# A four-layer hybrid decoder trunk: one more seven-product pair in three feed-forward blocks, and inverse roots by logarithm and exponential

## The chip, the cores and the metric

The kernel runs on 1 core of one Trainium2 chip. The metric is the device time of one execution in microseconds. Five engines work side by side, each through its own instruction list in order: TensorE (PE: matrix products; PEld is its weight load), VectorE (DVE), ScalarE (ACT), GpSimd (POOL) and SyncE (SP, which issues DMA transfers). They meet at semaphores: an instruction waits until a counter has reached a value, another adds to the counter when it is done.

## The reference

`x` has 512 tokens of 1024 features, float32. There are two layers, and each is `x + 0.5*FFN(norm(x))`, a token mixer, and another half-step FFN: four feed-forward blocks in all, numbered 0 to 3 here.

```
rms_norm(x, g)  = x * rsqrt(mean(x*x) + 1e-6) * g
swiglu(x)       = (silu(x @ w_gate) * (x @ w_up)) @ w_down      # 1024 -> 2816 -> 1024
layer 0 (even)  : FFN 0; dilated attention and causal pooling; FFN 1
layer 1 (odd)   : FFN 2; mLSTM, four heads, with an rms_norm of each head's output; FFN 3
```

## The kernel before

Features lie on the 128 partitions, tokens along the free dimension. All large products are float32 in accuracy: each operand is split into a high part (ScalarE copies it to the fp32r type: HI, XH, BF, ASH, HH) and a low part (value minus high part, on VectorE or GpSimd: LO, XL, BFL, ASL, HL), and three matmuls are summed: high by high, high by low, low by high.

**A feed-forward block** (`block_ffn(f, ...)`, written once for each engine) has 22 pairs of 128 hidden features. A pair has a gate and an up tile, `units` 2p and 2p+1, and each unit has 1024 input features, eight blocks of 128.

- A *plain* pair (p < `PLAIN[f]`) multiplies both units directly: 2 x 8 x 3 = 48 matmuls of 512 tokens (`products`, lines 579 to 581).
- A *block* pair (p >= `PLAIN[f]`) is a two by two product with seven multiplications instead of eight (`block(p)`, `product`, lines 656 to 658): 7 x 4 x 3 = 84 matmuls of 256 tokens. The halves are the input features and the tokens. Its tokens are sums of quarters of the normed x (`form`, `form_split`: BFR, BF, BFL, made once per FFN, four steps a = 0 to 3), and its weights are sums of quarter tiles in ASR, four per pair. Two of the four come from DMA: SP loads two quarters (`load_pair`), and GpSimd issues a transfer that adds the gate's left half to both (`add_pair`, an accumulating DMA, L2254). The other two are made on VectorE (`sums_second`, `sums_third`, L1664 and L1670). `sums_split(p, 0)` and `(p, 1)` make ASH on ScalarE and ASL on VectorE (L1676). After the products VectorE joins the partial results: `mid_two`, `mid_five`, `mid_three`, `whole_up`, `whole_gate`.
- In PE's order the seven products of a block pair are called here *one, seven, five, six, up-left, three, last*. *One* needs the pair's first LO (and, in the first block pair, all four split forms), *seven* needs `sums_split(p, 0)`, *six* needs `sums_split(p, 1)` and the copy of *one*, *last* needs `mid_two` and `mid_five` of the same pair.
- After every pair come `gate(p)` (bank times RSTD, VectorE), `silu(p)` (ScalarE), a product with RSTD (GpSimd, L2262, signals `sr_ready`), `up(p)` (VectorE, L1695), `h_high(p)` (ScalarE, L1179) and the low part HL on GpSimd (L2264).
- From a pair on, PE puts an *early* piece of the down projection behind each block pair (`early`, lines 709 to 711), with weights from DRAW/DHI/DLO (`load_early`, `early_split`). Its first pair is `PLAIN[f]`. The rest of the down projection follows at the end.

`PLAIN` is (5, 4, 3, 3): 17, 18, 19 and 19 block pairs, 73 in all.

**The norm.** The sum of squares is turned into a row on PE (L635, L636, into AUX, which is bank 4), behind the first three of eight steps of unit 2 or 3. ScalarE takes the root (L1123, `std_ready`), VectorE the reciprocal (L1610, `rstd_ready`). This is done six times. In the mLSTM a root (L1452) and a reciprocal (L2091) do the same for each of four heads. PE's first block pair waits for `std_ready` since product *seven* writes bank 4.

**What sets the order.** Every engine's list is written out by hand. The start of `block_ffn` has three variants: f == 0, f == 1 and the rest. In f = 2 and 3 the forms 0 and 1 are made behind the previous stage (`forms_behind`), forms 2 and 3 at the start of the block; in f = 1 all four are made at the start. Block 1 starts near 534 us, block 2 near 880 us, block 3 near 1606 us of the span.

## Time and profile before

| what | before |
|---|---|
| median of 3 runs | 1954.88 us (1954.53 to 1955.82) |
| the profiled execution's own time | 1955.77 us |
| its span, first to last instruction | 1954.0 us |
| PE busy | 1948.1 us, 100% |
| DVE busy | 1397.9 us, 72% |
| ACT busy | 851.6 us, 44% |
| POOL busy | 527.3 us, 27% |
| granted PE clock | 1.00 (2.4 GHz) |
| DMA | 265.92 MB, 136 GB/s |

A share of busy time is a mean over the whole span. PE's is a busy time with modelled ends, so starts of matmuls are the better measure of its pace. An instruction's duration in the timeline runs from its start to its visible end; the next one on the same engine can start about 0.08 us (VectorE) or 0.10 us (ScalarE) before that end.

### The profile page before, as it was taken

To read this page: it belongs to the slowest core of one execution; us is meant where nothing else is said; L and a number is where in the kernel's file an instruction comes from. 1 tells how busy PE (TensorE), PEld (TensorE's weight loads), DVE (VectorE), ACT (ScalarE), POOL (GpSimd) and SP (SyncE) were. 2 spreads that over 40 slices of the span, in tenths; PEclk is the share of its full clock that TensorE was granted. 3 is DMA by queue.
4 is the path that set the end of the run, shared out by engine and by line. 5 is a ranking of instruction groups with operands and counts; after the bars stand their busy time and mean duration, and the time that the engine had idled before them with its cause. 6 is when DMAs were issued, how large, how long until landed. Compare 5 with 4: busy or idle time off the path is not lost.

```text
span 1954.0 us, 28996 instructions
## 1 busy us (share of the span) xinstructions
PE 1948.1 (100%) x11722; PEld 1707.3 (87%) x11722; DVE 1397.9 (72%) x1882; ACT 851.6 (44%) x1230; POOL 527.3 (27%) x394
## 2 busy tenths in 40 slices
PE   9999999999999999999999999999999999999999
PEld 7999998877789999988999998877777888999997
DVE  7877776554588877768877776773458657877773
ACT  6443333535554344345433444442546345333431
POOL 1322222142223322223322322200015413322221
PEclk9999999999999999999999999999999999999999
DMA  6556663351346666545666653232200235666653
GB/s 211 155 164 171 173 168 95 119 181 55 88 126 176 174 172 167 147 129 145 178 166 172 181 151 114 97 96 88 76 1 1 87 116 160 177 173 168 178 141 107
DMA packets 112469, 265.92 MB, mean 136 GB/s; under 512 B 10321, under 2 KB 22865, under 8 KB 112337
## 3 DMA queue, kind: packets, MB, share of 16 engines
q1 hardware_dynamic: 92336, 225.72, 35.3%
q0 software_dynamic: 19856, 38.28, 12.5%
q8 instruction: 93, 1.52, 0.3%
q14 instruction: 40, 0.32, 0.0%
q10 hardware_dynamic: 144, 0.09, 0.0%
HBM read 259.32 MB, written 4.72 MB: 135 GB/s over the span
## 4 chain that ended last, share of the span: by engine, by line
PE 98%; DVE 1%; DMA 0%; issue 0%; ACT 0%; SPq 0%; POOL 0%; DVEq 0%
PE BANKS L656 12%; PE BANKS L658 12%; PE BANKS L657 12%; PE BANKS L579 11%; PE BANKS L580 11%; PE BANKS L581 11%; PE BANKS L709 6%; PE BANKS L710 6%; PE BANKS L711 6%; PE BANKS L1022 2%; PE BANKS L850 1%; PE BANKS L852 1%; PE BANKS L851 1%; PE BANKS L999 1%; PE BANKS L1005 1%; PE BANKS L813 1%
## 5 line engine op out<-in xcount | busy, mean ns | idle before, releaser
L656 PE MATMUL BANKS<-BF,ASH 128*128 128x256 f32 x876 | 248.0, 283 | 0.0
L658 PE MATMUL BANKS<-BF,ASL 128*128 128x256 f32 x876 | 247.9, 283 | 0.0
L657 PE MATMUL BANKS<-BFL,ASH 128*128 128x256 f32 x876 | 247.9, 283 | 0.0
L579 PE MATMUL BANKS<-XH,HI 128*128 128x512 f32 x624 | 245.7, 394 | 0.7 <-DVE XL L1593 0.3
L1657 DVE TENSOR_TENSOR LO<-RING,HI 128x1024 fp32r<-128x1024 f32 (+2 forms) x204 | 216.3, 1060 | 41.2 <-ACT HI L1160 39.9
L580 PE MATMUL BANKS<-XL,HI 128*128 128x512 f32 x624 | 243.2, 390 | 0.0
L581 PE MATMUL BANKS<-XH,LO 128*128 128x512 f32 x624 | 243.0, 389 | 0.0
L1173 ACT ACTIVATE TMP<-TMP 128x512 f32<-128x512 f32 x88 | 55.7, 633 | 406.4 <-DVE TMP L1686 406.4
L2262 POOL TENSOR_TENSOR TMP<-TMP,RSTD 128x512 f32<-128x512 f32 x88 | 132.0, 1499 | 365.3 <-ACT TMP L1173 365.3
L2254 POOL DMA_DIRECT2D ASR<-gu_dram x73 | 88.1, 1219 | 387.5 <-DMA ASR<-gu_dram 381.5
L709 PE MATMUL BANKS<-HH,DHI 128*128 128x512 f32 x488 | 190.7, 391 | 0.0
L710 PE MATMUL BANKS<-HL,DHI 128*128 128x512 f32 x488 | 190.6, 391 | 0.0
L1160 ACT ACTIVATE HI<-RING 128x1024 fp32r<-128x1024 f32 (+2 forms) x204 | 171.4, 876 | 42.3 <-DMA RING<-down_dram 21.4
L711 PE MATMUL BANKS<-HH,DLO 128*128 128x512 f32 x488 | 189.8, 389 | 0.0
L1676 DVE TENSOR_TENSOR ASL<-ASR,ASH 128x1024 fp32r<-128x1024 f32 x146 | 181.6, 1246 | 0.0
L2264 POOL TENSOR_TENSOR HL<-TMP,HH 128x512 fp32r<-128x512 f32 x88 | 139.0, 1580 | 146.6 <-ACT HH L1179 146.6
L1584 DVE TENSOR_TENSOR LO<-RING,HI 128x1024 fp32r<-128x1024 f32 x66 | 85.3, 1294 | 121.6 <-ACT HI L1102 121.5
L656 PEld LDWEIGHTS BANKS<-BF,ASH 128*128 128x128 f32 x876 | 168.2, 192 | 0.0
L657 PEld LDWEIGHTS BANKS<-BFL,ASH 128*128 128x128 f32 x876 | 168.2, 192 | 0.0
L658 PEld LDWEIGHTS BANKS<-BF,ASL 128*128 128x128 f32 x876 | 168.2, 192 | 0.0
L658 PE MATMUL BANKS<-XH,LO 128*128 128x256 f32 x584 | 165.3, 283 | 0.0
L657 PE MATMUL BANKS<-XL,HI 128*128 128x256 f32 x584 | 165.2, 283 | 0.0
(249 smaller groups left out, 4875.5 us busy)
## 6 DMA issues: line engine op xcount, KB each, us to landing
RING<-gu_dram SPq DMA_DIRECT2D x174, 512.0 KB, 3.9
ASR<-gu_dram SPq DMA_DIRECT2D x146, 256.0 KB, 2.9
ASR<-gu_dram POOLq DMA_DIRECT2D x73, 512.0 KB, 6.9
DRAW<-down_dram SPq DMA_DIRECT2D x40, 512.0 KB, 3.7
RING<-oin_dram SPq DMA_DIRECT2D x32, 512.0 KB, 3.5
RING<-down_dram SPq DMA_DIRECT2D x32, 384.0 KB, 3.2
DRAW<-down_dram SPq DMA_DIRECT2D x24, 384.0 KB, 3.7
RING<-ein_dram SPq DMA_DIRECT2D x16, 512.0 KB, 3.6
```

Of the source, the lines that this page charges most:

```text
L579: pe.matmul(PS[bank][:], HI[j][:, c], hi(k), start=(n == 0), stop=False)
L580: pe.matmul(PS[bank][:], HI[j][:, c], lo(k), start=False, stop=False)
L581: last = pe.matmul(PS[bank][:], LO[j][:, c], hi(k), start=False, stop=(n == len(order) - 1))
L656: pe.matmul(out, w_hi[:, c], x_hi(k), start=(k == 0), stop=False)
L657: pe.matmul(out, w_hi[:, c], x_lo(k), start=False, stop=False)
L658: last = pe.matmul(out, w_lo[:, c], x_hi(k), start=False, stop=(k == 3))
L709: pe.matmul(bank, DHI[:, col], HH[:, h % 8, :], start=(k == 0), stop=False)
L710: pe.matmul(bank, DHI[:, col], HL[:, h % 8, :], start=False, stop=False)
L711: last = pe.matmul(bank, DLO[:, col], HH[:, h % 8, :], start=False, stop=(h == tiles[-1]))
L1160: act.activation(HI[j][:, cols], RAW[j][:, cols], ACT.Copy).then_inc(hi_ready, 1)
L1657: dve.tensor_tensor(LO[j][:, cols], RAW[j][:, cols], HI[j][:, cols].bitcast(F32), ALU.subtract).then_inc(lo_ready, 1)
L1676: dve.tensor_tensor(ASL[:, p % 2, 2 * i:2 * i + 2, :], ASR[:, p % 2, 2 * i:2 * i + 2, :], ASH[:, p % 2, 2 * i:2 * i + 2, :].bitcast(F32), ...
```

## The change

- `PLAIN` becomes (5, 3, 2, 2): pair 3 of block 1 and pair 2 of blocks 2 and 3 become block pairs. A new tuple `EARLY_FROM = (5, 4, 3, 3)` keeps the first early piece of the down projection where it was, so the new block pair has none behind it.
- The lists at the start of blocks 1, 2 and 3 are reordered on ScalarE and VectorE. For the first block pair of these blocks the sums and splits of the next pair move (`ahead`), and its three `mid` steps stand ahead of the split of the next unit. In blocks 1 to 3 PE waits for the free gate bank ahead of product *five* instead of ahead of *one*.
- In blocks 2 and 3 the last `form_split` stands ahead of the norm on both engines.
- Block 2's first two accumulating transfers are issued by GpSimd between the squares of the previous block instead of after them.
- All norms and the head factor: `Sqrt` on ScalarE and `reciprocal` on VectorE become `Ln` and `Exp` with scale -0.5, both on ScalarE. `rstd_ready` takes the place of `std_ready` everywhere.

```diff
-PLAIN = (5, 4, 3, 3)
+PLAIN = (5, 3, 2, 2)
+EARLY_FROM = (5, 4, 3, 3)
...
@@ PE, block(p)
-                    pe.wait_ge(bank_free, n + 2)
+                    if f == 0:
+                        pe.wait_ge(bank_free, n + 2)
                     if p == PLAIN[f]:
-                        pe.wait_ge(std_ready, r + 1)
+                        pe.wait_ge(rstd_ready, r + 1)
...
                     product(PS[4][:, low], *summed(p, 0), form(1)).then_inc(seven_done, 1)
+                    if f:
+                        pe.wait_ge(bank_free, n + 2)
...
@@ ScalarE
             def norm(r):
                 act.wait_ge(norm_sum, r + 1)
-                act.activation(RSTD[:], AUX[:], ACT.Sqrt, scale=1.0 / DM, bias=EPST[:]).then_inc(std_ready, 1)
+                link(act.activation(RSTD[:], AUX[:], ACT.Ln, scale=1.0 / DM, bias=EPST[:]))
+                act.activation(RSTD[:], RSTD[:], ACT.Exp, scale=-0.5).then_inc(rstd_ready, 1)
...
@@ ScalarE, start of block 1
-                    split(6, whole)
                     silu(0, 1.0)
                     form_split(f, 3)
-                    split(7, whole)
+                    split(2 * first, whole)
+                    sums_split(first, 0)
                     h_high(0)
                     silu(1, 1.0)
-                    sums_split(first, 0)
+                    sums_split(first, 1)
+                    split(2 * first + 1, right)
                     h_high(1)
-                    silu(2, 1.0)
-                    split(2 * first, whole)
-                    h_high(2)
@@ ScalarE, start of blocks 2 and 3
                     form_inputs(f, 3)
+                    form_split(f, 3)
                     norm(now)
-                    split(4, whole)
-                    form_split(f, 3)
+                    split(2 * first, whole)
+                    sums_split(first, 0)
+                    sums_split(first, 1)
                     silu(0, 1.0)
-                    split(5, whole)
-                    sums_split(first, 0)
+                    split(2 * first + 1, right)
                     h_high(0)
...
@@ VectorE
             def norm(r):
-                dve.wait_ge(std_ready, r + 1)
-                dve.reciprocal(RSTD[:], RSTD[:]).then_inc(rstd_ready, 1)
                 dve.wait_ge(rstd_ready, r + 1)
@@ VectorE, start of block 1
                     form_split(f, 2)
-                    split(6, whole)
+                    sums_second(first)
+                    sums_third(first)
                     up(0)
                     gate(1)
                     form_split(f, 3)
-                    split(7, whole)
-                    up(1)
-                    gate(2)
-                    sums_second(first)
-                    sums_third(first)
-                    up(2)
@@ VectorE, start of blocks 2 and 3
                     form(f, 3)
+                    form_split(f, 3)
                     norm(now)
-                    split(4, whole)
                     gate(0)
-                    form_split(f, 3)
-                    up(0)
-                    split(5, whole)
-                    gate(1)
                     sums_second(first)
                     sums_third(first)
-                    up(1)
@@ VectorE, then in blocks 1 to 3
                 split(2 * first, whole)
                 sums_split(first, 0)
+                if f == 1:
+                    up(1)
                 sums_split(first, 1)
+                if f >= 2:
+                    up(0)
                 gate(first - 1)
                 split(2 * first + 1, right)
+                if f:
+                    sums_second(first + 1)
+                    sums_third(first + 1)
                 up(first - 1)
...
@@ GpSimd
+                    if f == 1 and m in (2, 3):
+                        add_pair(2, PLAIN[2] + m - 2)
```

## Rows read from the trace of the kernel before

**Rows 1.** The head of the page and its first part, busy times.
```profile
span 1954.0 us, 28996 instructions
PE 1948.1 (100%) x11722; PEld 1707.3 (87%) x11722; DVE 1397.9 (72%) x1882; ACT 851.6 (44%) x1230; POOL 527.3 (27%) x394
```
**Rows 2.** Waits of PE: line and releaser, us in total, times, longest.
```profile
PE BANKS L609 <- POOL HH L2330: 1.4, 1, 1.4
PE BANKS L1022 <- DVE VL L2108: 0.4, 1, 0.4
```
**Rows 3.** Timeline of PE in block 2: start, duration; operation; count.
```profile
902.35 0.39 PE L579 MATMUL BANKS<-XH,HI 128*128 128x512 f32 x1
...
913.23 0.28 PE L656 MATMUL BANKS<-XH,HI 128*128 128x256 f32 x1
...
923.30 0.40 PE L709 MATMUL BANKS<-HH,DHI 128*128 128x512 f32 x1
```
**Rows 4.** Groups of VectorE and ScalarE by line and shape: count, busy us, mean ns.
```profile
L1676 DVE TENSOR_TENSOR ASL<-ASR,ASH 128x1024 fp32r<-128x1024 f32 x146 | 181.6, 1246 | 0.0
...
L1686 DVE TENSOR_TENSOR TMP<-BANKS,RSTD 128x512 f32<-128x512 f32 x88 | 60.7, 690 | 2.5
...
L1657 DVE TENSOR_TENSOR LO<-RING,HI 128x512 fp32r<-128x512 f32 x73 | 49.7, 680 | 0.0
...
L1610 DVE RECIPROCAL RSTD<-RSTD 128x512 f32<-128x512 f32 x6 | 20.1, 3350 | 17.4 <-ACT RSTD L1123 17.4
...
L1160 ACT ACTIVATE HI<-RING 128x1024 fp32r<-128x1024 f32 x99 | 104.0, 1051 | 19.3 <-DMA RING<-gu_dram 8.6 <-DMA RING<-oin_dram 5.8 <-DMA RING<-ein_dram 4.9
L1173 ACT ACTIVATE TMP<-TMP 128x512 f32<-128x512 f32 x88 | 55.7, 633 | 406.4 <-DVE TMP L1686 406.4
```
**Rows 5.** Timeline of ScalarE at block 1's norm.
```profile
552.58 1.28 ACT L1123 ACT_TABLE_LOAD   x1
553.88 0.69 ACT L1123 ACTIVATE RSTD<-BANKS,EPST 128x512 f32<-128x512 f32 x1
...
558.44 1.28 ACT L1173 ACT_TABLE_LOAD   x1
```
**Rows 6.** Timeline of VectorE and GpSimd in block 1, 566 to 572 us.
```profile
566.05 1.21 DVE L1639 TENSOR_TENSOR BFL<-BFR,BF 128x1024 fp32r<-128x1024 f32 x1
...
566.27 2.14 POOL L2264 TENSOR_TENSOR HL<-TMP,HH 128x512 fp32r<-128x512 f32 x1 [3.90 <-ACT HH L1179]
...
567.18 2.31 DVE L1657 TENSOR_TENSOR LO<-RING,HI 128x1024 fp32r<-128x1024 f32 x1
...
568.37 2.27 POOL L2262 TENSOR_TENSOR TMP<-TMP,RSTD 128x512 f32<-128x512 f32 x1
570.67 0.69 DVE L1695 TENSOR_TENSOR TMP<-BANKS,TMP 128x512 f32<-128x512 f32 x1 [1.18 <-POOL TMP L2262]
```
**Rows 7.** Timeline of GpSimd, block 1, a product with VectorE idle.
```profile
581.98 1.29 POOL L2262 TENSOR_TENSOR TMP<-TMP,RSTD 128x512 f32<-128x512 f32 x1 [3.56 <-ACT TMP L1173]
```
**Rows 8.** Chain that ended last, around block 1's second block pair: start, us, what.
```profile
600.32 0.43 DVE MID L1701
...
600.77 0.43 DVE MID L1707
...
601.25 0.38 PE BANKS L656
```
**Rows 9.** Timeline of ScalarE in the mLSTM stage: an exponential, then a logarithm.
```profile
1383.01 0.63 ACT L1405 ACTIVATE TMP<-TMP 4x512 f32<-4x512 f32 x1
1383.65 1.28 ACT L1406 ACT_TABLE_LOAD   x1
```
**Rows 10.** Timeline of VectorE and ScalarE at the start of block 2.
```profile
894.69 0.42 DVE L1634 SCALAR_TENSOR_TENSOR BFR<-BFR,MID 128x256 f32<-128x256 f32 x1
...
898.83 1.06 ACT L1160 ACTIVATE HI<-RING 128x1024 fp32r<-128x1024 f32 x1 [4.00 <-DMA RING<-gu_dram]
```
**Rows 11.** Timeline of ScalarE at the start of block 3.
```profile
1619.60 0.69 ACT L1123 ACTIVATE RSTD<-BANKS,EPST 128x512 f32<-128x512 f32 x1 [4.47 <-PE BANKS L636]
1622.85 1.06 ACT L1160 ACTIVATE HI<-RING 128x1024 fp32r<-128x1024 f32 x1 [2.57 <-DMA RING<-gu_dram]
```

More of the change, by code:

```diff
@@ L287, in trunk @@
         sq_hi, sq_lo = sem("sq_hi"), sem("sq_lo")
-        norm_sum, std_ready, rstd_ready = sem("norm_sum"), sem("std_ready"), sem("rstd_ready")
+        norm_sum, rstd_ready = sem("norm_sum"), sem("rstd_ready")
         small_ready = sem("small_ready")
@@ L311, in trunk @@
         vh_ready, pth_ready, ptl_ready = sem("vh_ready"), sem("pth_ready"), sem("ptl_ready")
-        num_done, den_abs, num_sq, ssq_step, tstd_ready, num_read = (
-            sem(n) for n in ("num_done", "den_abs", "num_sq", "ssq_step", "tstd_ready", "num_read"))
+        num_done, den_abs, num_sq, ssq_step, factor_root, num_read = (
+            sem(n) for n in ("num_done", "den_abs", "num_sq", "ssq_step", "factor_root", "num_read"))
         column_sum, factor_ready, den_ready = sem("column_sum"), sem("factor_ready"), sem("den_ready")
@@ L364, in plain_bank @@
         def plain_bank(f, n):
-            return n + 1 if f < 2 and 4 <= n < 7 else n % 4
+            return n + 1 + f if f < 2 and 4 <= n < 7 - f else n % 4
         def block_count(f, p):
@@ L377, in early_index @@
         def early_index(f, p):
-            return p - PLAIN[f] - (p > ALONE[f])
+            return p - EARLY_FROM[f] - (p > ALONE[f])
         def has_early(f, p):
@@ L383, in leads @@
         def leads(f, p):
-            return has_early(f, p) and (p == PLAIN[f] or not has_early(f, p - 1))
+            return has_early(f, p) and not has_early(f, p - 1)
         def early_pairs(f):
@@ L461, in block_ffn @@
                     p = n // 2 - 1
-                    if n == plain + 1:
+                    if n == plain + 1 and has_early(f, PLAIN[f]):
                         load_early(PLAIN[f])
-                    elif n % 2 and p == ALONE[f]:
+                    elif n % 2 and p >= PLAIN[f] and leads(f, p + 1):
                         load_early(p + 1)
@@ L641, in bias_part @@
                     pe.wait_ge(bias_ready, 3)
-                    pe.wait_ge(std_ready, 2)
+                    pe.wait_ge(rstd_ready, 2)
                 if n >= 4:
@@ L1252, in block_ffn @@
                     form_inputs(f, 3)
+                    form_split(f, 3)
                     norm(now)
-                    split(4, whole)
-                    form_split(f, 3)
+                    split(2 * first, whole)
+                    sums_split(first, 0)
+                    sums_split(first, 1)
                     silu(0, 1.0)
-                    split(5, whole)
-                    sums_split(first, 0)
+                    split(2 * first + 1, right)
                     h_high(0)
-                    silu(1, 1.0)
-                    split(2 * first, whole)
-                    h_high(1)
-                sums_split(first, 1)
-                split(2 * first + 1, right)
+                if f == 0:
+                    sums_split(first, 1)
+                    split(2 * first + 1, right)
                 silu(first - 1, 1.0)
@@ L1268, in block_ffn @@
                     copy_one(p)
-                    if p == first:
+                    ahead = f and p == first
+                    if f and p == first + 1:
+                        silu(p - 1, -1.0)
+                    if ahead:
+                        split(2 * nxt, whole)
+                        sums_split(nxt, 0)
+                        sums_split(nxt, 1)
+                    if not has_early(f, p - 1):
                         h_high(p - 1)
+                    if p == first and has_early(f, p):
                         early_split(p)
-                    elif not has_early(f, p - 1):
-                        h_high(p - 1)
-                    if nxt:
+                    if ahead:
+                        split(2 * nxt + 1, right)
+                    elif nxt:
                         split(2 * nxt, whole)
@@ L1281, in block_ffn @@
                         split(NU + 1, late)
-                    if p == ALONE[f]:
+                    if leads(f, p + 1):
                         early_split(p + 1)
@@ L1285, in block_ffn @@
                         early_split(p)
-                    silu(p, -1.0)
+                    if not ahead:
+                        silu(p, -1.0)
                     if has_early(f, p):
@@ L1451, in root @@
                         act.wait_ge(factor_ready, h + 1)
-                        act.activation(RSTD[:], RSTD[:], ACT.Sqrt).then_inc(tstd_ready, 1)
+                        link(act.activation(RSTD[:], RSTD[:], ACT.Ln))
+                        act.activation(RSTD[:], RSTD[:], ACT.Exp, scale=-0.5).then_inc(factor_root, 1)
                 def square_numerator(h, c):
@@ L1853, in block_ffn @@
                     elif nxt:
-                        sums_second(nxt)
-                        sums_third(nxt)
+                        if p == first:
+                            mid_two(p)
+                            mid_five(p)
+                            mid_three(p)
+                        else:
+                            sums_second(nxt)
+                            sums_third(nxt)
                         dve.wait_ge(sum_made, 2 * block_count(f, nxt) + 2)
                         split(2 * nxt, whole)
-                        mid_two(p)
-                        mid_five(p)
-                        mid_three(p)
+                        if p > first:
+                            mid_two(p)
+                            mid_five(p)
+                            mid_three(p)
                         sums_split(nxt, 0)
@@ L2087, in head_factor, with root_ready @@
                                              ALU.add).then_inc(factor_ready, 1)
-                def invert_factor(h):
-                    dve.wait_ge(tstd_ready, h + 1)
-                    link(dve.reciprocal(RSTD[:], RSTD[:]))
+                def root_ready(h):
+                    dve.wait_ge(factor_root, h + 1)
                 def scale_numerator(h, c):
@@ L2142, in odd_mixer @@
                     value_low(h, 2)
-                    invert_factor(h - 1)
+                    root_ready(h - 1)
                     weighted(h, 0)
```

23 lines of the change are left out of this document (12 added, 11 removed).

## The prediction

> **What bounds the kernel now.** First the page's busy shares: PE is busy for 1948.1 of 1954.0 us, VectorE for 72% [rows 1]. Then PE's waits: the two longest are 1.4 us at the very start and 0.4 us in the mLSTM stage [rows 2]. So no wait of any size can be removed; time comes only out of PE's own work, and every microsecond by which another engine makes PE wait is added in full. Third, PE's pace by starts: from 902.35 to 913.23 lie the 48 matmuls of one plain pair, 10.88 us (0.227 each); from 913.23 to 923.30 the 84 of a block pair, 10.07 us (0.120 each) [rows 3]. The last view is the chain around PE's one wait inside the feed-forward blocks: in block 1 VectorE's `mid_five` ends at 601.20 and PE's product *last*, whose predecessor started at 600.90, starts at 601.25 instead of 601.02 [rows 8]. There VectorE is the engine that comes late, just behind the stretch where the change puts more on it.
>
> **The gain.** Three pairs change kind: 3 x (10.88 - 10.07) = 2.43 us less PE work. It is there only if the inputs come in time. Each new block pair starts 10.88 us earlier than the first one did: at 567.25 (578.13 - 10.88) in block 1, 902.35 in block 2, 1628.27 in block 3.
>
> **The work added.** A plain pair costs VectorE two splits of 1.14 us and two bank reads of 0.60 (next start after the durations of rows 4, less 0.08): 3.5. A block pair costs it one and a half splits (1.74), two sums (1.32), two sum splits (2.28), three mids (1.15), two joins (1.3), two bank reads (1.2): 9.0. So +5.5 us of VectorE per changed pair, -3.35 for the reciprocal [rows 4]. The form steps (1.53 each, 1.14 for each split) stay in the same stretch.
>
> **The root.** Before: table load, Sqrt 0.69, reciprocal 3.35 on VectorE. After: Ln 0.69, another table load 1.28, Exp about 0.65. That the pair needs two loads I read from the mLSTM stage, where an Exp is followed at once by a load of 1.28 us for the Ln [rows 9]. RSTD is there 2.7 us after the sum instead of 4.4: 1.7 earlier; but ScalarE is later by 1.9 us, and VectorE, freed of 3.35 us, waits for ScalarE instead. The Trainium skill (ScalarE: Activation LUTs, "Table sets: the hidden batching unit") says that ln and then exp cost one load, since one set has both. The trace has a case in the other order only, with two loads. By the skill's rule each norm would be 1.3 us shorter: a rival, below.
>
> **The meeting with GpSimd.** At 566.27 a GpSimd operation starts while a VectorE split is under way until 567.18: it takes 2.14 us, against 1.29 when VectorE is idle [rows 6, 7]. VectorE's next split, 567.18, takes 2.31 instead of 1.21, and ends 1.1 us behind GpSimd's end at 568.41; GpSimd's next, from 568.37, takes 2.27 [rows 6]. So these two take turns when VectorE's operands lie in SBUF, and each turn lost costs 1.2 us. Reads of a bank don't show it. I lay the new order out with that, instruction by instruction, in the durations above. The same layout of the old order puts block 1's second block pair at 592.7 (592.4 in the trace), so I trust it to some 0.3 us per block.
>
> **Block 1, laid out.** Ln starts at 553.88 like the Sqrt [rows 5], load to 555.9, Exp to 556.5, the high part of unit 5 (1.05) to 557.4. VectorE: LO of unit 5 to 558.6, gate 0 to 559.2, form 3 to 560.7, form split 2 to 561.8; the two sums of pair 3 with one lost turn to 564.3; up 0 and gate 1 to 565.5; form split 3 to 566.7; then LO of unit 6, behind GpSimd's HL 0, to 569.0. PE wanted it at 567.25: **1.8 us**. The first sum split loses the next turn (sr 1) and ends at 571.3, *seven* wanted it at 570.5: 0.9. ScalarE copies *one* only behind silu 2, which waits for gate 2 at 573.6: *six* is 0.5 late. Then the next pair's split and sum split, behind `mid_three`: *seven* of pair 4 is 0.6 late. `mid_five` of pair 4: 0.36, of pair 5: 0.31. Sum 4.4 (4.38), against 0.56 in my layout of the old order, less 0.81 for the pair: **+3.0 us**. The moved wait for the gate bank costs nothing: up 1 ends at 571.9, *five* starts at 572.8.
>
> **Block 2.** Form 3 ends at 895.11 [rows 10]. ScalarE's last form split now stands ahead of the norm, so it waits for that until 895.15, ends at 896.1, and only then come load, Ln, load, Exp: RSTD at 900.1, where the old order had it at 898.4. Here the new root is later, not earlier. Gate 0, two sums, LO of unit 4: 903.3; PE wanted it at 902.35: **1.0 late**. ScalarE: high part of unit 4, two sum splits, silu's table load, silu 0 at 904.4, GpSimd's product to 906.7, up 0 to 907.4: *five* wanted it at 906.2: **1.3 late**. Then *six* 0.1, `mid_five` 0.4, and LO of unit 6, which loses a turn to HL 1, 1.1; in the next two pairs 0.1 and 0.3. Sum 4.2 - 0.81 = **+3.4 us**. The two accumulating transfers that go out sooner should take away ScalarE's 4.00 us of waiting for unit 4's weights, which ended at 898.83 [rows 10]; but ScalarE gets to this split only at 900.0. Worth 0 here, and 0 if the weights come as late as before.
>
> **Block 3.** The same lists, but form 3 is ready 3 us before the norm's sum, which comes at 1619.6 [rows 11]. Ln, load and Exp end at 1622.2; unit 4's weights landed at 1622.85 before [rows 11] and set ScalarE's start. LO of unit 4 at 1625.4 (wanted 1628.3), up 0 at 1629.7 (wanted 1631.1): both in time. Only LO of unit 6 is 0.24 late, and the mids 0.37. 0.6 - 0.81 = **-0.2 us**.
>
> **The rest.** Block 0's norm: VectorE freed, ScalarE 1.9 us later, hidden under its wait of 2 us for weights behind it: 0. The norms ahead of the mixers: 0, PE reads RSTD's result 6 us later at least. mLSTM roots: ScalarE's value copy comes 1.9 us later and is read in time by 0.3 us, VectorE loses 3.35 us of work per head; PE waits there for neither: 0, between -0.5 and +1. A table load more for the q/k root falls into idle time: 0. PE's wait for `rstd_ready` instead of `std_ready`: 10 us early in block 1, 2.2 in block 2, covered by LO.
>
> **Sum.** +3.0 + 3.4 - 0.2 = +6.2 us. Against the profiled execution's 1955.77 (span 1954.0, 1.77 around it) that is 1962.0 us, span 1960.2. The median of the runs is 0.89 lower, so the forecast is **1961.1 us**. What a measurement can tell from no change is 0.2%, 3.9 us: 1951.0 to 1958.8.
>
> **Rivals.**
> - *The turns don't fall on the path (not slower).* VectorE and GpSimd take turns as in rows 6, but in the new order GpSimd's operations slip into VectorE's waits. For: the reciprocal goes, and in the trace many GpSimd operations meet an idle VectorE [rows 7]. Against: in block 1 VectorE now has no gap between 557 and 587. With no lost turn in either order the layout gives -0.8, +1.3, -0.8, and the old order's 0.4 us of stall goes: -0.7, 1954.2 us. It decides from the point where LO of unit 6 (block 1) is there by 567.3. Chance 0.17.
> - *All arrives in time.* -2.43 and the old stalls of 0.4: 1952.1 us. For it block 2's form 3 would have to be ready sooner too, and nothing in the change does that. Chance 0.05.
> - *Ln and Exp in one table set.* RSTD 1.3 us earlier, by the layout +1.75 in block 1 and +2.1 in block 2, -0.2 in block 3: +3.7, 1958.5 us. Against it stand rows 9. This is the skill's rule named above. Chance 0.08.
> - *Block 3 goes like block 2.* The weights of unit 4 or the sums of pair 2 land later than the 1622.85 of rows 11, since the pair's accumulating transfers are issued at the old place there, and the pair starts 10.88 us sooner. From 2.9 us of delay on PE waits. At block 2's price, +9.8 in all: 1964.7 us. Chance 0.12.
> - The forecast: 0.56, own range 1959 to 1963.5. The rest, 0.02, is beyond all of these.
>
> Range 1953.8 to 1964.8: it takes in the first, third and fourth rival. Faster by over 0.2%: 0.05 (the second rival with gains in the mixers I don't see). Within 0.2%: 0.17 + 0.05 and the larger part of the one-set case, with the forecast's lower tail: 0.31. Slower: 0.64.
>
> **What would show it.** In the profile after: 84-matmul stretches of 10.07 us from pair 3, 2 and 2 on; a table load between Ln and Exp at each norm; PE waiting on LO near 567 and 903 for 1 to 2 us and on up 0 near 906; the start of block 1's pair 6 near 609.9 (606.9 before) and of block 2's pair 5 some 3.4 us later again; none of it in block 3; no new waits in the mixers. It is wrong if PE's first block pair of block 1 starts within 0.3 us of 567.25, if the load between Ln and Exp is missing, or if VectorE's split of unit 6 runs undisturbed.

## The result, and the profile after

The changed kernel takes 1964.07 us (median of 5 runs, 1962.99 to 1964.44) against 1955.08 for the kernel before (5 runs); the ratio is 1.0043, 95% interval 1.0031 to 1.0055, that is 6 to 11 us more. Forecast were 1961.1, range 1953.8 to 1964.8, slower with chance 0.64: the direction and the main mechanism are right, the size is 3.0 us short. The number lies above the forecast's own range (1959 to 1963.5) and close to the 1964.7 of the rival on block 3; what tells the two apart is the table of stages below, not the number. The profiled execution is the shortest of the five, 1962.99, with a span of 1961.3 (1954.0 before).

First the head and the busy times of the page after, beside [rows 1], and PE's waits after (line and releaser, us in total, times, longest), beside [rows 2]:

```profile
span 1961.3 us, 29291 instructions
PE 1949.0 (99%) x11830; PEld 1711.4 (87%) x11830; DVE 1388.9 (71%) x1899; ACT 875.0 (45%) x1258; POOL 533.1 (27%) x397
```
```profile
PE BANKS L657 <- DVE LO L1667: 2.7, 2, 1.4
PE BANKS L610 <- POOL HH L2345: 1.4, 1, 1.4
PE BANKS L657 <- DVE ASL L1686: 1.3, 3, 0.5
PE BANKS L657 <- DVE TMP L1705: 1.0, 1, 1.0
PE BANKS L657 <- DVE MID L1717: 0.5, 3, 0.2
```

VectorE has 9 us less work than before, and this execution is 7.3 us longer: its reciprocals are gone, but the work that was added is due sooner. The waits stand where the prediction put them: the splits LO of block 1 and block 2 (2.7 us), up 0 (1.0), the sum splits (1.3), the mids. The timeline of PE shows the four long ones (start, duration, operation, idle time ahead of it and what ended it):

```profile
567.71 0.39 PE L657 MATMUL BANKS<-XH,HI 128*128 128x256 f32 x1 [1.39 <-DVE LO L1667]
...
569.93 0.38 PE L657 MATMUL BANKS<-BF,ASH 128*128 128x256 f32 x1 [0.54 <-DVE ASL L1686]
...
906.88 0.39 PE L657 MATMUL BANKS<-XH,HI 128*128 128x256 f32 x1 [1.33 <-DVE LO L1667]
...
911.02 0.39 PE L657 MATMUL BANKS<-BF,ASH 128*128 128x256 f32 x1 [1.00 <-DVE TMP L1705]
```

The scale for all that follows is PE's own timeline. I take the start of the same matmul in both traces (the norm matmuls, and one *early* matmul well inside each feed-forward block) and subtract. How much the distance grows from one mark to the next is what a stage costs, freed of how the execution began (up to the middle of block 0 every other kernel here is 0.5 to 1.2 us ahead of the profiled execution of before). In us, pairs of marks in order of time:

```
                  block 1   1 to 2   block 2   mLSTM   block 3
forecast            +3.0      0        +3.4      0      -0.2
changed kernel      +2.9     +1.2      +3.9     +0.5    -0.2
```

"1 to 2" runs from the early pairs of block 1 to block 2's norm. Two measures of a wait are used below: the idle time of the profile's rows, and the distance of two starts of PE less the usual 0.12 or 0.23 us, which comes out some 0.16 us longer for the same wait (1.39 and 1.55 on LO in block 1). In block 1 all such excesses of starts come to 4.2 us against 0.4 before; less the pair's 0.81 that is the +2.9. Two terms that stood in the sum with 0 are not 0 (1 to 2 and mLSTM), and they are the larger part of what was missing.

The second table load is there at each of the six norms. ScalarE at block 2's norm, after:

```profile
898.51 1.06 ACT L1146 ACTIVATE BF<-BFR 128x1024 fp32r<-128x1024 f32 x1 [2.33 <-DVE BFR L1644]
899.59 1.28 ACT L1127 ACT_TABLE_LOAD   x1
900.88 0.69 ACT L1127 ACTIVATE RSTD<-BANKS,EPST 128x512 f32<-128x512 f32 x1
901.59 1.28 ACT L1128 ACT_TABLE_LOAD   x1
902.88 0.63 ACT L1128 ACTIVATE RSTD<-RSTD 128x512 f32<-128x512 f32 x1
```

The step is as forecast: the form split stands ahead of the norm and waits 2.33 us for VectorE. The splits that lose their turn to GpSimd in block 1 are there too. VectorE, then GpSimd:

```profile
565.34 2.31 DVE L1667 TENSOR_TENSOR LO<-RING,HI 128x1024 fp32r<-128x1024 f32 x1
567.58 2.31 DVE L1686 TENSOR_TENSOR ASL<-ASR,ASH 128x1024 fp32r<-128x1024 f32 x1
...
564.43 2.14 POOL L2277 TENSOR_TENSOR HL<-TMP,HH 128x512 fp32r<-128x512 f32 x1 [2.62 <-ACT HH L1184]
566.52 2.27 POOL L2275 TENSOR_TENSOR TMP<-TMP,RSTD 128x512 f32<-128x512 f32 x1
```

### The profile page after: what moved, and what is told of

The parts are those of the page before. It is cut to its first block and busy times, and to the rows that moved or that the text cites. A ratio compares the mean times of both kernels' runs of the same rounds, so it can differ in the third digit from the quotient of the medians.

```text
span 1961.3 us, 29291 instructions
## 1 busy us (share of the span) xinstructions
PE 1949.0 (99%) x11830; PEld 1711.4 (87%) x11830; DVE 1388.9 (71%) x1899; ACT 875.0 (45%) x1258; POOL 533.1 (27%) x397
## 5 line engine op out<-in xcount | busy, mean ns | idle before, releaser
L657 PE MATMUL BANKS<-BF,ASH 128*128 128x256 f32 x912 | 258.9, 284 | 2.5 <-DVE ASL L1686 1.3
L659 PE MATMUL BANKS<-BF,ASL 128*128 128x256 f32 x912 | 258.1, 283 | 0.0
L658 PE MATMUL BANKS<-BFL,ASH 128*128 128x256 f32 x912 | 258.1, 283 | 0.0
L580 PE MATMUL BANKS<-XH,HI 128*128 128x512 f32 x576 | 227.0, 394 | 1.0 <-DVE LO L2210 0.3
L581 PE MATMUL BANKS<-XL,HI 128*128 128x512 f32 x576 | 224.6, 390 | 0.0
L582 PE MATMUL BANKS<-XH,LO 128*128 128x512 f32 x576 | 224.3, 389 | 0.0
L1686 DVE TENSOR_TENSOR ASL<-ASR,ASH 128x1024 fp32r<-128x1024 f32 x152 | 189.9, 1251 | 0.0
L657 PEld LDWEIGHTS BANKS<-BF,ASH 128*128 128x128 f32 x912 | 175.0, 192 | 3.6 <-DVE ASL L1686 1.9
L658 PEld LDWEIGHTS BANKS<-BFL,ASH 128*128 128x128 f32 x912 | 175.1, 192 | 0.0
L657 PE MATMUL BANKS<-XH,HI 128*128 128x256 f32 x608 | 171.9, 283 | 2.7 <-DVE LO L1667 2.7
```

Of the source, the lines that this page charges most:

```text
L580: pe.matmul(PS[bank][:], HI[j][:, c], hi(k), start=(n == 0), stop=False)
L581: pe.matmul(PS[bank][:], HI[j][:, c], lo(k), start=False, stop=False)
L582: last = pe.matmul(PS[bank][:], LO[j][:, c], hi(k), start=False, stop=(n == len(order) - 1))
L657: pe.matmul(out, w_hi[:, c], x_hi(k), start=(k == 0), stop=False)
L658: pe.matmul(out, w_hi[:, c], x_lo(k), start=False, stop=False)
L659: last = pe.matmul(out, w_lo[:, c], x_hi(k), start=False, stop=(k == 3))
```

## The experiments

Five kernels take the change apart, four alter one thing in the changed kernel, two follow from what these showed, and one repeats the changed kernel. All but the last are built with three switches: `NEW` names the blocks whose pair changes kind (a block that isn't in it keeps the old order), `ROOT` chooses the roots, `SOONER` the place of the transfers. The code shown is what is different in effect, shortened at each `...`; the lines of the switches themselves stand there only where they say it best. Runs of before beside them: 1955.1 to 1955.5 us, medians of 15 to 21.

### The parts

**The accumulating transfers at their old place**, the rest of the change kept.

```diff
-                if f != 2:
-                    for p in (PLAIN[f], PLAIN[f] + 1):
-                        add_pair(f, p)
+                for p in (PLAIN[f], PLAIN[f] + 1):
+                    add_pair(f, p)
...
-                    if f == 1 and m in (2, 3):
-                        add_pair(2, PLAIN[2] + m - 2)
```

> The changed kernel with one part undone: GpSimd issues block 2's first two accumulating transfers again behind all eight squares of block 1. My theory: in the changed kernel the two issues at 873.6 and 875.6 us hold GpSimd between the squares and stretch two VectorE steps (2.77 and 2.15 us), so VectorE is late at the start of block 2 and PE waits twice there (0.4 and 0.35 us excess). Undone, block 2's norm comes 1.2 us sooner relative to block 1's last pair, about as in the kernel before, and the rest of block 2 stays at +3.9 us: total 1.2 us less than the changed kernel (about 1962.5 to 1963). Rival: the weights of unit 4 come later then and cost as much or more in block 2 as was won: total unchanged or up to 1 us more.

Measured: 1961.86 us, ratio 1.0035 [1.0023, 1.0048]. By stages: block 1 +2.5, 1 to 2 **0.0**, block 2 +3.5, mLSTM +0.5, block 3 -0.3. So issuing them sooner costs 1.2 us between the blocks and buys nothing in block 2. (Block 1, the same code, differs by 0.4; see the landings below.)

**The roots alone**: old pairs, old transfers, Ln and Exp everywhere.

```diff
-PLAIN = (5, 3, 2, 2)
+NEW = ()
+ROOT = 'exp'
+SOONER = False
+PLAIN = tuple(n - (f in NEW) for f, n in enumerate((5, 4, 3, 3)))
```

> The kernel before with the roots alone changed: Ln and Exp instead of Sqrt and reciprocal, PLAIN and all orders as before. My layout: the 0.4 us of waits in block 1 go (-0.5 us), blocks 2 and 3 unchanged, +0.3 to +0.5 us in the mLSTM stage, where ScalarE's copy of v2 comes 1.9 us later: within 0.5 us of the kernel before. Rival: the second table load is what costs the changed kernel its time; then this one is 3 us or more slower than before.

Measured: 1955.14 us, ratio 1.0000 [0.9991, 1.0010]. Block 1 -0.4, mLSTM +0.5, the rest within 0.1.

**Block 3's pair alone**, with the new roots and the old transfers.

```diff
-PLAIN = (5, 3, 2, 2)
+NEW = (3,)
+ROOT = 'exp'
+SOONER = False
+PLAIN = tuple(n - (f in NEW) for f, n in enumerate((5, 4, 3, 3)))
```

> The changed kernel with blocks 1 and 2 as before (4 and 3 plain pairs, old orders) and the transfers at the old place; only block 3 has its new block pair, and the roots are Ln and Exp. My layout: block 3 -0.2 us, roots as in the run beside it: 1954.4 to 1955.2, no difference to before that can be measured, and the whole loss of the changed kernel gone. Rival: block 3 loses time too once it isn't hidden behind a later start: 1957 or more.

Measured: 1954.93 us, ratio 1.0000 [0.9990, 1.0009]. Block 1 -0.3, mLSTM +0.5, block 3 +0.25 with three PE waits of 0.2 to 0.3 us. Even here, where nothing is late by more than that, small waits pay the pair's 0.81 us [rows 3] back.

**The change with Sqrt and reciprocal kept.**

```diff
-                link(act.activation(RSTD[:], AUX[:], ACT.Ln, scale=1.0 / DM, bias=EPST[:]))
-                act.activation(RSTD[:], RSTD[:], ACT.Exp, scale=-0.5).then_inc(rstd_ready, 1)
+                act.activation(RSTD[:], AUX[:], ACT.Sqrt, scale=1.0 / DM, bias=EPST[:]).then_inc(std_ready, 1)
...
+                dve.reciprocal(RSTD[:], RSTD[:]).then_inc(rstd_ready, 1)
```

> The changed kernel with Sqrt and reciprocal put back in all norms and the head factor, the rest of the change kept. My layout: block 1 +3.9 instead of +3.0 us, block 2 +4.8 instead of +3.4, block 3 +1.0 instead of -0.2, mLSTM 0.5 less: 3.0 us slower than the changed kernel, about 1967. Rival (the extra table load harms more than the reciprocal): 1 us or more faster than the changed kernel.

Measured: 1967.26 us (1966.92 to 1967.59), ratio 1.0061 [1.0045, 1.0078]; block 1 +4.6, 1 to 2 +1.2, block 2 +5.3, mLSTM 0, block 3 +1.2. PE waits 3.2 us at 566.5 and 2.9 at 907.4, both for LO. So within the change the new roots save 3.2 us (1967.26 - 1964.07), and they do so only because the new pairs have put the norm on the path; alone they are worth 0. Part of block 1's difference is its landing, the latest of all (542.1 on the scale used below): the kernel whose weights landed at 542.0 costs +3.9 there, so the roots' share is about 0.7. The layout had no term for one thing that the trace shows here alone: behind these two waits, in which PE stood idle for 3.08 and 2.75 us, the granted clock is 0.53 (569.9 to 573.5) and 0.59 (910.5 to 914.7), so PE runs mostly at the lower level, 1.2 GHz, and its matmuls start 0.21 us apart instead of 0.12. By the starts that is some 1.5 us each time. Most of it hides waits that would have come next: those of 0.70 and 0.30 us in block 1 and of 1.16 in block 2 are gone. In the changed kernel, idle for 1.39 and 1.33 us at these places, the clock stays at 1.00.

**The transfers alone**, in the kernel before.

```diff
-                for p in (PLAIN[f], PLAIN[f] + 1):
+                if f != 2:
+                    for p in (PLAIN[f], PLAIN[f] + 1):
                         add_pair(f, p)
...
+                    if f == 1 and m in (2, 3):
+                        add_pair(2, PLAIN[2] + m - 2)
```

> The kernel before with one part of the change only: block 2's first two accumulating transfers are issued among the last squares of block 1. Theory 'issuing them stretches VectorE': VectorE's LO and XL splits beside the two issues near 873 and 875 take 2 to 3 us instead of 1.1 and 0.8, PE waits 0.4 us twice near 881 and 886, and the stretch from the last early pair of block 1 to block 2's first norm matmul costs +1.2 us; block 2 itself gains nothing, since its waits are none in the kernel before: 1956.3 us against 1955.1. Rival 'the +1.2 comes from the new order of block 1': that stretch costs 0 here, 1955.1 us.

Measured: 1956.50 us, ratio 1.0007 [0.9998, 1.0016]; too little for the whole time, but the stage says it: 1 to 2 +1.1, block 2 0.0 (and block 1, whose code is that of before, +0.4). How it comes about stands in VectorE's and GpSimd's timeline. First the changed kernel, then, for the same two VectorE operations, the kernel with the transfers back:

```profile
874.30 2.77 DVE L1667 TENSOR_TENSOR LO<-RING,HI 128x896 fp32r<-128x896 f32 x1
876.99 2.15 DVE L1605 SCALAR_TENSOR_TENSOR XL<-X,PAR,XH 128x512 fp32r<-128x512 f32 x1
...
873.58 1.21 POOL L2265 DMA_DIRECT2D ASR<-gu_dram  x1 [6.85 <-DMA ASR<-gu_dram]
874.35 1.76 POOL L2252 TENSOR_TENSOR SQ<-SQ,TMP 128x512 f32<-128x512 f32 x1
875.59 1.67 POOL L2265 DMA_DIRECT2D ASR<-gu_dram  x1
876.37 2.22 POOL L2252 TENSOR_TENSOR SQ<-SQ,TMP 128x512 f32<-128x512 f32 x1
```
```profile
873.90 1.08 DVE L1707 TENSOR_TENSOR LO<-RING,HI 128x896 fp32r<-128x896 f32 x1
874.90 0.74 DVE L1642 SCALAR_TENSOR_TENSOR XL<-X,PAR,XH 128x512 fp32r<-128x512 f32 x1
```

Two splits grow from 1.8 to 4.9 us. The first transfer waits for the weights that it adds to (6.85 us), and the square behind it is held up until both squares and both issues fall on VectorE's splits in one piece. Of these 3.1 us VectorE's idle time behind them takes up 1.6, and PE waits 0.4 us near 882 and 887 for LO and XL, besides smaller ones. In the kernel with the transfers alone it isn't the same two operations:

```profile
871.53 1.08 DVE L1707 TENSOR_TENSOR LO<-RING,HI 128x896 fp32r<-128x896 f32 x1
872.53 2.00 DVE L1642 SCALAR_TENSOR_TENSOR XL<-X,PAR,XH 128x512 fp32r<-128x512 f32 x1
874.89 1.85 DVE L1677 SCALAR_TENSOR_TENSOR BFR<-X,PAR,MID 128x256 f32<-128x256 f32 x1 [0.36 <-ACT MID L1148]
...
871.44 1.21 POOL L2333 DMA_DIRECT2D ASR<-gu_dram  x1 [7.50 <-DMA ASR<-gu_dram]
872.22 1.76 POOL L2320 TENSOR_TENSOR SQ<-SQ,TMP 128x512 f32<-128x512 f32 x1
873.72 1.42 POOL L2333 DMA_DIRECT2D ASR<-gu_dram  x1
874.50 1.96 POOL L2320 TENSOR_TENSOR SQ<-SQ,TMP 128x512 f32<-128x512 f32 x1
```

Here LO, which was expected to take 2 to 3 us, starts beside the first issue and takes its 1.08; stretched are XL and the form step (0.48 in the kernel before), which meet the two squares. The changed kernel's whole trace agrees that an issue alone takes nothing from VectorE: 67 splits of 128x1024 run while GpSimd has nothing but an issue under way, and they take 1.21 to 1.23 us each, as the 147 with GpSimd idle do. So what the issues do is to hold the squares back and to lengthen them (1.76 to 2.22 us behind an issue, 1.46 without), and it is the squares that VectorE loses to.

### One thing changed in the changed kernel

**Fewer GpSimd columns in block 2.**

```diff
-                    pool.tensor_tensor(HL[:, p % 8, :], SG[:, p % 2, :], HH[:, p % 8, :].bitcast(F32),
+                    cut = slice(0, 8 if f == 2 and p <= 4 else T)
+                    pool.tensor_tensor(HL[:, p % 8, cut], SG[:, p % 2, cut], HH[:, p % 8, cut].bitcast(F32),
```

> In block 2, GpSimd's subtraction for HL of pairs 0 to 4 takes 8 columns instead of 512 (it leaves out the low part of h there); all else as in the changed kernel, whose block 2 costs 3.9 us more than the kernel before's (906.9 to 942.9: PE waits of 1.33 on LO of unit 4, 1.00 on up 0, 0.54 on the sum split, 0.2 and 0.3). Theory 'turns' (a VectorE operation on SBUF that meets one of GpSimd loses 1.2 us): the layout without these GpSimd operations gives +1.6 for block 2, and the waits behind up 0 (sum split, mids) go, while LO of unit 4 and up 0 stay, since no HL runs before them. Rival 'VectorE has too much to do': HL is not VectorE's work, so block 2 stays at +3.6 to +4.1. Whole kernel: 1961.8 by the theory, 1964.0 by the rival.

Measured: 1962.12 us, ratio 1.0039 [1.0026, 1.0051]. Block 2 +2.3 instead of +3.9. In block 2 PE's waits of 0.71, 0.20 and 0.33 us behind up 0 are gone, those on LO (1.58) and up 0 (1.15) stay. (Waits here are by starts.) VectorE's work is the same in both, so the 1.6 us are turns lost to GpSimd. The layout gave +1.6 for the whole block, so it took off 0.7 us too much. In the profiled execution block 1 (same code) took +3.9; why is told below.

**The norm first in block 2.**

```diff
-                    form_split(f, 3)
-                    norm(now)
+                    if f == 2:
+                        norm(now)
+                        form_split(f, 3)
...
-                    form_split(f, 3)
-                    norm(now)
-                    gate(0)
+                    if f == 2:
+                        norm(now)
+                        gate(0)
+                        form_split(f, 3)
```

> In block 2 alone, ScalarE does the norm's Ln and Exp ahead of the last form split, and VectorE gate 0 ahead of its half of that split. Theory 'the form split holds the root up': RSTD is there 1.0 us or more sooner, PE's wait on up 0 near 910 goes or falls below 0.3 us, and block 2 costs +1.5 instead of +3.9 by the layout: 1961.6 us. Rival 'GpSimd and VectorE decide from here': the root comes sooner but up 0 and LO of unit 4 are as late as before, since form split 3 now stands between: +3.5 to +4, 1964 us.

Measured: 1961.93 us, ratio 1.0034 [1.0022, 1.0047]. Block 2 +2.0, where the layout gave +1.5: the wait on LO is gone, up 0 is 0.8 late instead of 1.2 (expected: below 0.3), the sum split 0.7 as in the changed kernel. So the place of the form split costs 1.9 us; the rest goes only with the new order below. Block 3, whose code was not touched, costs +0.66 in this execution; see block 3 below. ScalarE in this kernel, to be held beside the five rows above (Exp ended at 903.51 there and ends at 899.85 here, 3.7 us sooner, 0.2 of them because PE itself is sooner):

```profile
897.22 0.69 ACT L1134 ACTIVATE RSTD<-BANKS,EPST 128x512 f32<-128x512 f32 x1
897.93 1.28 ACT L1135 ACT_TABLE_LOAD   x1
899.22 0.63 ACT L1135 ACTIVATE RSTD<-RSTD 128x512 f32<-128x512 f32 x1
899.76 1.04 ACT L1153 ACTIVATE BF<-BFR 128x1024 fp32r<-128x1024 f32 x1
```

**No second table load.**

```diff
-                link(act.activation(RSTD[:], AUX[:], ACT.Ln, scale=1.0 / DM, bias=EPST[:]))
+                link(act.activation(RSTD[:], AUX[:], ACT.Exp, scale=1.0 / DM, bias=EPST[:]))
```

> In the six norms of model width, ScalarE's Ln is replaced by an Exp on the same operands, so that Exp follows Exp and no table is loaded between them (the root computed is not the reference's). It prices the second table load. Theory: RSTD comes 1.28 us sooner at each norm; by the layout block 1 costs +1.75 instead of +3.0 forecast (2.9 measured) and block 2 +2.1 instead of 3.4 (3.9 measured), block 3 and the mixers the same: 1961.5 us. Rival 'RSTD is not what is late': VectorE's LO of unit 6 in block 1 and of unit 4 in block 2 wait for VectorE's own list, so the waits stay and the kernel gains less than 0.5 us: 1963.6 us.

Measured: 1960.09 us, ratio 1.0027 [1.0016, 1.0038]. Block 1 +1.2, block 2 +2.6, both 1.3 less than with the load (block 1 against executions with the same landing, below). PE's waits on LO go in both blocks and those on up 0 and the sum splits stay. By the stages a load of 1.28 us costs 1.3 us of the kernel's time twice, and nothing at the other four norms. The whole time fell by 4.0 us, to below the 1961.5 expected; the stages of the one profiled execution account for 2.7 of them, and where the rest is stays open.

**Block 2's start in another order.**

```diff
+                    norm(now)
+                    form_split(f, 3)
+                    split(2 * first, whole)
+                    sums_split(first, 0)
+                    silu(0, 1.0)
+                    sums_split(first, 1)
+                    split(2 * first + 1, right)
+                    h_high(0)
...
+                        sums_second(first)
+                        sums_third(first)
+                        norm(now)
+                        gate(0)
+                        form_split(f, 3)
...
+                    sums_second(first + 1)
+                    sums_third(first + 1)
+                    up(0)
+                    gate(first - 1)
+                    sums_split(first, 1)
+                    up(first - 1)
+                    split(2 * first + 1, right)
```

> Block 2's start in another order, all else as in the changed kernel: ScalarE norm, form split 3, unit 4, sum split 0, silu 0, sum split 1, unit 5, h 0; VectorE the sums of pair 2, gate 0, form split 3, LO of unit 4, sum split 0, the sums of pair 3, up 0, gate 1, sum split 1, up 1, LO of unit 5. Theory 'it is the order, not the amount of work': the layout gives -0.6 for block 2 (all in time), against 3.9 measured in the changed kernel: 1959.6 us. Rival 'a third block pair this early is too much for VectorE and GpSimd in any order': LO of unit 4 stays late by 1 us or more, or the waits move to five and seven; block 2 at +2 or more, 1962 us or above.

Measured: 1959.84 us (1959.4 lowest), ratio 1.0024 [1.0014, 1.0034]. Block 2 **-0.15** instead of +3.9: of its waits one of 0.33 us on a mid is left. VectorE and GpSimd around the place where PE waited 1.3 and 1.0 us in the changed kernel:

```profile
902.79 1.22 DVE L1719 TENSOR_TENSOR LO<-RING,HI 128x1024 fp32r<-128x1024 f32 x1
903.93 1.22 DVE L1738 TENSOR_TENSOR ASL<-ASR,ASH 128x1024 fp32r<-128x1024 f32 x1
905.07 0.68 DVE L1726 TENSOR_TENSOR ASR<-ASR,RING 128x512 f32<-128x512 f32 x1
...
907.38 0.68 DVE L1757 TENSOR_TENSOR TMP<-BANKS,TMP 128x512 f32<-128x512 f32 x1
...
905.54 1.36 POOL L2371 TENSOR_TENSOR TMP<-TMP,RSTD 128x512 f32<-128x512 f32 x1 [13.54 <-ACT TMP L1185]
```

Same instructions, same loads, other order: all of block 2's cost was order. The layout had promised 0.4 us more (-0.6).

### What the runs pointed to

**Block 3's pair alone, reordered, Sqrt in the mLSTM heads.** Roots and transfers as said in the expectation, `PLAIN` as in block 3's pair alone. The start of block 3 on ScalarE, then on VectorE:

```diff
+                    sums_split(first, 0)
                     form_split(f, 3)
                     norm(now)
                     split(2 * first, whole)
-                    sums_split(first, 0)
+                    silu(0, 1.0)
                     sums_split(first, 1)
-                    silu(0, 1.0)
+                    h_high(0)
                     split(2 * first + 1, right)
-                    h_high(0)
...
-                sums_split(first, 1)
...
                     up(0)
...
+                    sums_split(first, 1)
```

> What the runs so far leave of the change: the pair changes kind in block 3 alone, whose start is reordered (ScalarE: sum split 0, form split 3, norm, unit 4, silu 0, sum split 1, h 0, unit 5; VectorE: up 0 ahead of sum split 1); Ln and Exp in the six norms; Sqrt and reciprocal kept in the mLSTM heads; the accumulating transfers at their old places. By the layout: block 1 -0.4, block 3 -0.8, mLSTM 0: 1953.9 us against 1955.1. Rival 'the pair in block 3 gives nothing in any order' (it gave +0.25 alone and -0.22 in the changed kernel): 1954.7. Rival 'the 0.5 us in the mLSTM stage is not from the roots there': 1954.4.

Measured: 1956.34 us (1956.04 to 1956.96), ratio 1.0005 [0.9996, 1.0014]. A miss: block 3 costs +1.7 where the layout gave -0.8. mLSTM 0.0, block 1 -0.4, as expected; block 2, whose pairs are the old ones, +0.3. What the layout missed, VectorE and GpSimd:

```profile
1626.86 2.32 DVE L1726 TENSOR_TENSOR ASL<-ASR,ASH 128x1024 fp32r<-128x1024 f32 x1
...
1626.63 1.47 POOL L2347 TENSOR_TENSOR TMP<-TMP,RSTD 128x512 f32<-128x512 f32 x1 [12.47 <-ACT TMP L1185]
```

With silu 0 moved forward, GpSimd's first product starts 0.23 us ahead of the sum split instead of behind it, takes the turn, and PE waits 0.7 us on that split and 0.3, 0.4, 0.2 and 0.3 after it: the same row of waits as in block 1.

**The norms' roots alone.** Old pairs, old transfers, Ln and Exp in the six norms, Sqrt and reciprocal in the heads.

```diff
-                        link(act.activation(RSTD[:], RSTD[:], ACT.Ln))
-                        act.activation(RSTD[:], RSTD[:], ACT.Exp, scale=-0.5).then_inc(factor_root, 1)
+                        act.activation(RSTD[:], RSTD[:], ACT.Sqrt).then_inc(factor_root, 1)
...
+                        link(dve.reciprocal(RSTD[:], RSTD[:]))
```

> The kernel before with Ln and Exp in the six norms only; the mLSTM heads keep Sqrt and reciprocal, the pairs and the accumulating transfers stay as before. With all roots changed, block 1 gave back 0.39 us and the mLSTM stage cost 0.49. Theory 'the mLSTM cost is the roots there': block 1 -0.4, mLSTM 0, the rest 0: 1954.8 us against 1955.2, too little for the whole time to tell and to be read from the stages. Rival 'it is scatter between executions': the mLSTM stage costs 0.3 to 0.5 again, or block 1 gives nothing.

Measured: 1954.90 us (11 runs) beside 1955.51, ratio 0.9996 [0.9987, 1.0005]. Block 1 -0.3, mLSTM 0.0. The shortest median of all, and no difference that can be measured.

**The changed kernel once more.**

> The changed kernel itself once more, to see how far its stages scatter between executions. Kernels with the same code in block 1 cost 2.5 to 3.9 us there. Theory 'the turns fall differently from one execution to the next': block 1 between +2 and +4 with the wait on LO of unit 6 between 0.9 and 2.5 us, while the waits that follow from ScalarE's and GpSimd's chain in block 2 (LO of unit 4, up 0) repeat within 0.2 us. Rival 'an execution of the same kernel repeats its waits': every stage within 0.2 us of +2.9, +1.2, +3.9, +0.5, -0.2. Whole kernel 1963 to 1965 us.

Measured: 1963.88 us, ratio 1.0040 [1.0024, 1.0055], profiled span 1962.7. Block 1 +3.5, 1 to 2 +1.3, block 2 +3.9, mLSTM +0.5, block 3 -0.2, and 0.3 us in the stage ahead of block 1. Of the five stages only block 1 differs by more than 0.2 us between these two executions of one kernel. My theory on it (the turns fall differently) is wrong: the turns are the same ones. ScalarE's first split of block 1, here and in the two executions at either end:

```profile
541.26 1.06 ACT L1106 ACTIVATE HI<-RING 128x1024 fp32r<-128x1024 f32 x1 [4.08 <-DMA RING<-gu_dram]
```
```profile
539.46 1.06 ACT L1110 ACTIVATE HI<-RING 128x1024 fp32r<-128x1024 f32 x1 [2.70 <-DMA RING<-gu_dram]
```
```profile
541.02 1.06 ACT L1110 ACTIVATE HI<-RING 128x1024 fp32r<-128x1024 f32 x1 [4.23 <-DMA RING<-gu_dram]
```

(the repetition; the norm first; fewer GpSimd columns). What differs is when the weights land. The split waits for a weight transfer, and from it to the start of LO of unit 6 there are 25.4 us (25.6 with the transfers back) of ScalarE and VectorE work with no gap that gives way: 565.34 - 539.94 in the changed kernel, 566.67 - 541.26, 564.92 - 539.46, 566.42 - 541.02. Put on PE's clock of before (by PE's shift at the block's norm), the split starts at 540.4 with the transfers back, 540.5 with the norm first, 541.0 in the changed kernel, 541.6 with the new order, 541.7 in the repetition and 542.0 with fewer columns, and PE is idle for 0.95, 0.95, 1.39, 1.96, 2.00 and 2.32 us ahead of the product that needs LO: nearly one for one. Block 1 as a whole costs 2.5, 2.5, 2.9, 3.5, 3.5 and 3.9 us in the same order. Without the second load the chain is 24.1 us.

## Why the prediction was right, and short

- **The bound and the gain.** Right. PE had nothing to give back but its own work, and the late inputs were added. PE's operations are busy 0.9 us longer than before (more, shorter instructions), while their starts are closer. The pairs' gain of 0.81 us each is in every stage's sum, but no run collects all of it: in block 2's new order, with -0.15, a wait of 0.33 us and smaller ones are left.
- **Block 1, +3.0.** Measured +2.9 and +3.5. The step "LO of unit 6: 1.8 us" was 1.4 and 2.0; *seven* 0.9 was 0.7; *six* 0.5 was 0.3; *seven* of pair 4, 0.6, was 0.4; the mids 0.7 were 0.5. The layout started from the one landing that the trace before showed, 541.3, and for that one its 1.8 us on LO fits what the six executions show (1.4 at 541.0, 2.0 at 541.6). But block 1 goes from +2.5 to +3.9 in executions of the same code, in the order of their landings, and I gave that no term and no width. That +3.0 lies so near +2.9 is luck to that extent.
- **Block 2, +3.4.** Measured +3.9 twice, +3.5 with the transfers back. The cause was named rightly: form split 3 holds the root. With the norm ahead of it the stage costs 2.0, without the second load 2.6, without GpSimd's HL 2.3. LO of unit 4 (1.0 forecast) was 1.3 of idle time, up 0 (1.3) 1.0, the sum split 0.5 where I had 1.1 on LO of unit 6.
- **Accumulating transfers, "worth 0".** This step failed: 1.2 us too little. I asked only what ScalarE's wait of 4.00 us [rows 10] was worth at the receiving end. I had not asked what the two issues do where they are put, between GpSimd's squares and beside VectorE's splits, though the same turn-taking [rows 6] was the core of my argument elsewhere. The transfers alone and the transfers back show it from both sides: the issue, held until its weights are there (6.85 us), moves the squares onto VectorE's splits.
- **mLSTM, 0, between -0.5 and +1.** Measured +0.5 in each kernel with Ln and Exp there, 0.0 in those without. The end that I took was wrong, its range right. PE waits 0.3 us near 1491 and 1518, since VectorE's scaling of the numerator comes late, behind GpSimd's YL. GpSimd, VectorE, PE:

```profile
1484.03 0.29 POOL L2342 TENSOR_SCALAR_AFFINE_SELECT TMP<-TMP 128x128 f32<-128x128 f32 x1 [1.44 <-ACT TMP L1486]
...
1489.24 1.29 POOL L2337 TENSOR_TENSOR YL<-TMP,YH 128x512 fp32r<-128x512 f32 x1
```
```profile
1490.57 0.75 DVE L2108 SCALAR_TENSOR_TENSOR TMP<-BANKS,PAR,RSTD 128x512 f32<-128x512 f32 x1 [0.76 <-POOL YL L2337]
```
```profile
1491.38 0.50 PE L1056 MATMUL BANKS<-PTH,VH 128*128 128x512 f32 x1
```

  GpSimd works from 1484.03 to this YL with gaps of at most 0.2 us, and there it had waited 1.44 us for ScalarE's exponentials (L1486), which stand behind Ln, load and Exp. I had followed the value copy, which is read in time, not what stands behind it. On PE's clock of before they and this first GpSimd operation start 0.5 us later than they did (before: 1476.56 on GpSimd; PE is 6.95 us later here), which is the size of the loss. It is the added Exp and not a table load: in the kernel before each head has two loads too, one for Sqrt and one for these exponentials. That these exponentials are the cause is argued from the rows; the runs show only that the 0.5 us come and go with the roots in the heads.
- **Block 3, -0.2.** Measured -0.2 in both executions of the changed kernel, but +0.1 and +0.66 in two others with the same code there, +0.25 with its pair alone and +1.7 in the other order. Here too it goes by the landing of unit 4's weights, on PE's clock of before: at 1622.4 to 1622.7 the block costs -0.2 or -0.3, at 1623.0 (block 2's new order) +0.1, at 1623.6 (the norm first in block 2) +0.66. The prediction said that PE waits only from 2.9 us of delay on; the runs show it from some 0.1 on. So its rival that block 3 goes like block 2 didn't come true in the changed kernel, but its condition, a late landing, is near: the figure was right with a thin margin.
- **The one-set rival** (1958.5). Refuted by the rows: twelve loads at the six norms. Its price came out near: +1.75 and +2.1 by the layout, +1.2 (at an early landing) and +2.6 measured, 1960.1 us in all with the transfers' 1.2 in it. The Trainium skill (ScalarE: Activation LUTs, "Table sets: the hidden batching unit") puts ln and exp in one load; in this trace Ln to Exp costs a load of 1.28 us as Exp to Ln did [rows 9].
- **The sum.** 3.0 us short: 1.2 (transfers), 0.5 (mLSTM), 0.5 (block 2); the other 0.8 wasn't taken apart. It is no more than executions differ by: the stages of the profiled one, the shortest of its five, sum to +8.3, those of the repetition to +9.0.

## What to carry to other kernels

Where PE is the bound and the others run just ahead, moving a step earlier moves a chain of fixed length closer to whatever starts it (a landing, a norm): find that chain, take its length from the trace, and price the change from there, with the landing's scatter as its width. An instruction that is moved "for free" to another place of GpSimd's list is to be priced where it lands, by what VectorE does beside it. And try the order first: block 2's new pair cost 3.9 us or nothing, with the same instructions.

## What the runs showed of the hardware

- With two accumulating transfers issued between GpSimd's squares, VectorE's splits beside them grow from 1.08 and 0.74 to 2.77 and 2.15 us. The issue alone does nothing to a VectorE split (67 of them at 1.21 to 1.23 us); the squares that it holds back do.
- A lost turn costs a VectorE split of 128x1024 1.1 us (2.32 against 1.22 us), and who starts first decides it: in block 3's other order GpSimd was 0.23 us ahead.
- Ln and then Exp cost a table load of 1.28 us between them, each of six times at the norms and four in the heads.
- The landing of block 1's first weight transfer scatters by 1.6 us between executions against PE's clock, that of block 3's unit 4 by 1.2. It costs nothing as long as its chain has room, and then nearly one for one.
- After 3.08 and 2.75 us without a matmul the granted clock was 0.53 and 0.59 over the next 3.6 and 4.2 us; after 1.39 and 1.33 us it stayed at 1.00.
